# Keeping one product of a gated merge in its PSUM bank, in a one-core transformer-layer kernel

## The reference, cut to what matters

```python
z = rms_norm(x, g_mix) @ w_in                     # p, q, k, v, gate_pool, gate_attn
y_pool = pool_mixer(p, w_pool_grp, pool_scale) @ w_branch_pool
y_attn = window_attention(q, k, v, sinks) @ w_branch_attn
merged = sigmoid(gate_pool) * y_pool + sigmoid(gate_attn) * y_attn
x = x + merged @ w_out
x = x + peer_layer(rms_norm(x, g_ffn), ...)       # keys, top 16, 128 experts for each token
out = rms_norm(x, g_final)
```

## Time and profile before

| | |
|---|---|
| median of 3 runs | 2860.17 us |
| lowest and highest run | 2859.67, 2865.98 us |
| span of the profiled execution | 2856.4 us |
| merge loop, first pass | about 142 to 254 us |
| output projection, first pass | about 254 to 298 us |
| merge loop, second pass | about 542 to 653 us |
| output projection, second pass | about 653 to 699 us |

### The profile page before, as it was taken

The page is one execution under the profiler, slowest core; times in us unless marked ns, Lnnn a source line. Parts: engine busy times, 40 slices in busy tenths (PEclk is TensorE's granted clock), DMA queues, the critical chain, the costliest instruction groups (busy, mean ns, idle before and its releaser), DMA issues.

```text
span 2856.4 us, 39882 instructions
## 1 busy us (share of the span) xinstructions
PE 2772.4 (97%) x14843; PEld 2411.2 (84%) x14843; DVE 2332.4 (82%) x4690; ACT 964.2 (34%) x1505; POOL 2035.7 (71%) x1541
## 2 busy tenths in 40 slices
PE   8999999999998999999999999999999999999997
PEld 6688787687887888889988998999899989988996
DVE  2622798685899996888899998888898988989998
ACT  4432443324322996222222232222222222222222
POOL 5444478386786997687778777877677777778774
PEclk9999999999998999999999999999999999999999
DMA  4123422133323778899989988999899889989995
GB/s 155 46 88 96 170 75 82 40 105 107 107 92 123 227 231 300 306 346 348 339 324 358 345 330 332 351 348 335 322 350 345 330 338 343 353 315 361 336 349 205
DMA packets 267728, 717.90 MB, mean 251 GB/s; under 512 B 20880, under 2 KB 104208, under 8 KB 267536
## 3 DMA queue, kind: packets, MB, share of 16 engines
q0 software_dynamic: 110912, 403.75, 37.3%
q1 hardware_dynamic: 156624, 311.61, 32.4%
HBM read 657.86 MB, written 57.41 MB: 250 GB/s over the span
## 4 chain that ended last, share of the span: by engine, by line
PE 35%; DVE 6%; DMA 5%; POOL 2%; issue 1%; ACT 1%; DVEq 0%; SPq 0%; ACTq 0%
PE abank L1759 6%; PE abank L1761 6%; PE abank L1760 6%; PE ybank L1775 6%; PE ybank L1774 6%; PE ybank L1776 6%; DVE acc L1936 3%; DMA up<-in_up,e_idx 3%; DMA up<-in_down,e_idx 2%; DVE up L1924 1%; POOL tdown_lo L1706 1%; DVE e_y L2010 1%; POOL up L1699 1%; DMA w<-all_pre 1%; ACT tdown_hi L1800 0%
## 5 line engine op out<-in xcount | busy, mean ns | idle before, releaser
L1759 PE MATMUL abank<-m_hT,tdown_hi 128*128 128x384 f32 (+1 forms) x1856 | 579.4, 312 | 11.8 <-DVE w_lo L2002 6.8
L1761 PE MATMUL abank<-m_hT,tdown_lo 128*128 128x384 f32 (+1 forms) x1856 | 578.6, 312 | 0.0
L1760 PE MATMUL abank<-m_hlo,tdown_hi 128*128 128x384 f32 (+1 forms) x1856 | 577.7, 311 | 0.0
L1936 DVE SCALAR_TENSOR_TENSOR acc<-up,e_act,acc 128x1024 f32<-128x1024 f32 x381 | 489.8, 1286 | 70.0 <-DMA up<-in_up,e_idx 51.5
L1924 DVE CUSTOM_DVE_ANT_0 up<-up,acc 128x1024 f32<-128x1024 f32 x384 | 455.4, 1216 | 81.2 <-DMA up<-in_down,e_idx 80.6
L1774 PE MATMUL ybank<-tup_hi,w_hi 128*128 128x512 f32 x1280 | 503.5, 393 | 14.0 <-DVE w_lo L2002 10.5
L942 POOL TENSOR_TENSOR m_wlo<-m_raw,m_whi 128x1024 fp32r<-128x1024 f32 x128 | 311.5, 2442 | 288.2 <-ACT m_whi L719 284.6
L1775 PE MATMUL ybank<-tup_lo,w_hi 128*128 128x512 f32 x1280 | 502.7, 393 | 0.0
L1776 PE MATMUL ybank<-tup_hi,w_lo 128*128 128x512 f32 x1280 | 502.2, 392 | 0.0
L1699 POOL DMA_INDIRECT up<-in_down,e_idx x384 | 363.7, 947 | 99.1 <-issue 79.2
L1699 POOL DMA_INDIRECT up<-in_up,e_idx x384 | 362.2, 943 | 99.2 <-issue 80.6
(11 more groups left out here) (245 smaller groups left out, 4509.6 us busy)
## 6 DMA issues: line engine op xcount, KB each, us to landing
e_tup<-in_up SPq DMA_DIRECT2D x128, 512.0 KB, 5.5
m_raw<-in_tiles SPq DMA_DIRECT2D x116, 512.0 KB, 3.5
e_tdown<-in_downT SPq DMA_DIRECT2D x116, 512.0 KB, 5.5
gates<-all_table SPq DMA_DIRECT2D x64, 640.0 KB, 4.5
all_table<-t_out SPq DMA_DIRECT2D x9, 4096.0 KB, 14.6
m_raw<-in_downT SPq DMA_DIRECT2D x12, 512.0 KB, 3.8
up<-in_down,e_idx POOLq DMA_INDIRECT x384, 6.5
up<-in_up,e_idx POOLq DMA_INDIRECT x384, 6.5
```

The lines of the kernel that those rows point to most:

```text
L1759: nc.tensor.matmul(out, tdown_hi[:, q, at], h2T_hi[:, k, a:b], start=k == 0, stop=False)
L1760: nc.tensor.matmul(out, tdown_hi[:, q, at], h2T_lo[:, a:b, at], start=False, stop=False)
L1761: ins = nc.tensor.matmul(out, tdown_lo[:, q, at], h2T_hi[:, k, a:b], start=False, stop=k == KD - 1)
L1936: ins = nc.vector.scalar_tensor_tensor(out=acc[:], in0=src, scalar=act_of[:, b, k:k + 1], in1=acc[:], op0=ALU.mult, op1=ALU.add)
```

## The change

The product of the pool branch is written back to its own PSUM bank rather than to `sg[:, m % 2, 0]`. The sum is made in that bank too, and both the high and the low part of `merged` are taken from it. The product of the attention branch goes to `sg[:, m % 2, 1]` as before. Two waits follow from this. The bank of `bp` is now in use until the low part is taken, so its release is `m_low` and no longer `merged`. The sigmoids of step m overwrite what step m-2 had in `sg`, and that is now last read by the sum, so they wait for `merged` of step m-2 rather than for `m_low`.

```diff
         for m in range(KD):
             for i, name in enumerate(("gp", "ga")):
                 frees[name, m] = (sig_ready, 2 * m + 1 + i, 2 * KD) if m > 1 else (early_kept, 2 * m + 1 + i, TT)
-            frees["bp", m] = frees["ba", m] = (merged, m + 1, KD)
+            frees["bp", m] = (m_low, m + 1, KD)
+            frees["ba", m] = (merged, m + 1, KD)
...
-                    nc.scalar.activation(mhi(m), sg[:, m % 2, 0], ACT.Copy).then_inc(m_high, 1)
+                    nc.scalar.activation(mhi(m), bank("bp", m)[:], ACT.Copy).then_inc(m_high, 1)
...
                         if m >= 2:
                             wait_job(act, g, n, m)
-                            act.wait_ge(m_low, g * KD + m - 1)
+                            act.wait_ge(merged, g * KD + m - 1)
...
                 def merge_low(m):
                     dve.wait_ge(m_high, g * KD + m + 1)
-                    nc.vector.tensor_tensor(mlo[:, m], sg[:, m % 2, 0], mhi(m).bitcast(F32), ALU.subtract).then_inc(m_low, 1)
+                    nc.vector.tensor_tensor(mlo[:, m], bank("bp", m)[:], mhi(m).bitcast(F32), ALU.subtract).then_inc(m_low, 1)
 
                 for m in range(KD):
                     for i, n in enumerate(("bp", "ba")):
                         wait_job(dve, g, n, m)
                         dve.wait_ge(sig_ready, g * 2 * KD + 2 * m + 1 + i)
-                        mark(nc.vector.tensor_tensor(sg[:, m % 2, i], bank(n, m)[:], sg[:, m % 2, i], ALU.mult))
+                        to = sg[:, m % 2, 1] if i else bank(n, m)[:]
+                        mark(nc.vector.tensor_tensor(to, bank(n, m)[:], sg[:, m % 2, i], ALU.mult))
                     linked()
-                    nc.vector.tensor_tensor(sg[:, m % 2, 0], sg[:, m % 2, 0], sg[:, m % 2, 1], ALU.add).then_inc(merged, 1)
+                    nc.vector.tensor_tensor(bank("bp", m)[:], bank("bp", m)[:], sg[:, m % 2, 1], ALU.add).then_inc(merged, 1)
```

## The result

| | before | after |
|---|---|---|
| median of 20 runs | 2859.51 us | 2865.15 us |
| lowest to highest run | 2854.86 to 2865.98 us | 2861.14 to 2869.17 us |
| ratio to before, 95% interval | | 1.0023 [1.0016, 1.0029] |
| span of the profiled execution | 2856.4 us | 2859.4 us (its own time: 2861.44 us) |

By the medians the change makes the kernel slower by 5.6 us; the ratio stands for 6.6 us, its interval for 4.6 to 8.3 us. The forecast was 2865.3 us, no change within 0.3%, on the slow side. The profiled execution is the second shortest of the 20, so its span must not be set against the medians; what it is good for is the places.

What follows compares the result with a forecast made beforehand. TensorE's matmul stream was taken as the bound. Stalls of 0.88 and 2.53 us plus 1.70 us of clock gave 5.1 us, on a base of 2860.2 us: 2865.3 us, range 2859 to 2870 us.

Steps and rivals of the forecast that it cites:

- Nothing inside the loop: Merge loop, both passes: the new waits for low parts and the earlier sigmoids change nothing on TensorE, 0 us.
- First stall, 0.88 us: Start of first pass's output projection: output job (1,0) waits for low part 6, +0.88 us.
- Second stall, 4.06 us against 1.53 us: Second pass's output projection: job (1,0) waits 4.06 us for low part 6, replacing 1.53 us at job (3,0), +2.53 us.
- The clock, 1.70 us: Behind the second pass's stall: TensorE's granted clock dips once to the lower level, +1.70 us.
- rival B: End of second pass: VectorE arrives earlier; 2861.1 us if by 2.5 us, 2859.5 us if by 4.1 us; chance 0.14.
- PSUM operands at 0.69 us, free of GpSimd: Merge steps on VectorE: sum and low part with one operand in PSUM take 0.69 us, without waiting for GpSimd.
- Rival C: Both loop ends: sum and low part still wait for GpSimd; 9.5 us with a clock dip, 2869.7 us; chance 0.05.
- The sum, 5.1 us: TensorE's stream over both passes: 0.88 + 2.53 + 1.70 = 5.1 us longer in all.
- Slack behind it: Norm, turning, projections and the two stages after the output jobs: no slack, so the whole shift reaches the end.

Runs made afterwards that it cites:

- experiment 2: Changed kernel with low part 6 taken at the end of step 6, ahead of the products of step 7; 2858.82 us, ratio 0.9999 to before.
- experiment 6: Changed kernel with the output jobs at k = 0 alone in token order 0, 2, 1, 3; 2859.16 us, ratio 0.9995 to before.
- experiment 1: Kernel before with only the release of bp's bank moved from the sum to the low part, all data in SBUF; 2868.59 us, ratio 1.0034.
- experiment 3: Changed kernel with output jobs at k = 0 and 1 reordered, tokens 0 and 2 first, then 1 and 3; 2857.00 us, second timing 2856.07 us.
- 7: Changed kernel with low part 6 computed seven times in the second pass; 2868.53 us, ratio 1.0030 to before.
- 9: Changed kernel with low part 6 computed twice in both passes; 2864.53 us, ratio 1.0014 to before.
- experiment 4: Kernel before with output jobs at k = 0 and 1 reordered, tokens 0 and 2 first, then 1 and 3; 2859.05 us, ratio 0.9999.

## Why the prediction was right

*Nothing inside the loop.* Right: no wait for line 1292 but the two at the ends, and the freed sigmoids brought nothing.

*First stall, 0.88 us.* Measured 0.87 us in both profiles.

*Second stall, 4.06 us against 1.53 us.* Measured 3.80 and 3.82 us, so +2.3 in place of +2.5 us. The mechanism was right; the term was off by VectorE's arrival, which I had taken as fixed: it comes 2.53 us after TensorE's first output matmul now and came 2.78 us after it before. Its lookup instructions meet GpSimd's at slightly other moments (next to GpSimd's last weight copy it is the CAST of line 1164 that takes 2.40 us before, and now the later one of line 1169 that takes 2.32 us); this is rival B, at a tenth of its size.

*The clock, 1.70 us.* Right in both profiles of the changed kernel. That it was a forecast with a chance of its own was right too: experiment 2 kept its clock with 1.71 us of idle, 6 lost it with 2.27, and in 1 it stayed at 1.00 after 2.86 us in the first pass. But the row that the term was taken from proved less than I read out of it. TensorE starts the expert loop behind the same 2.84 us of idle in all 13 profiles of this study, and the clock fell behind it in six of them (among them before and the first profile after) and not in the other seven, as here in the second profile of experiment 3:

```profile
1101.19 0.36 PE L1763 MATMUL abank<-m_hT,tdown_hi 128*128 128x256 f32 x1 [2.84 <-PEq L1392]
...
1102.00:1107.00 5.00, 5.00 (x37) 1.00 1.14 346
```

For an idle stretch of 2.84 us the dip is a toss-up. Behind the longer stalls at (1,0) it came each time, 3.64 to 7.99 us in five profiles of five, so the term stands on the length of the stall; its size, 1.7 us, was the same in both places.

*PSUM operands at 0.69 us, free of GpSimd.* Right in 64 of 64, products included. By an estimate from the Trainium skill's larger fixed cost for a PSUM source (VectorE: DVE Perf Modes, section on the TRN2 errata), sum and low part would each have taken 0.065 us more; the sum took 0.700 us with all but one operand in PSUM against 0.691 us at least in SBUF, so the trace still does not agree. The Trainium skill (SBUF — State Buffer, section "SBUF: two separate sides") names as the VectorE instructions that take the port pair shared with GpSimd those in a 2-port mode and those with two SBUF inputs, the latter only against a GpSimd instruction that reads SBUF. The trace agrees: with one SBUF input 0.70 us at most, with two up to 2.97 us. Rival C, that they stay held, was wrong; its price was about right, since experiment 1 has it: 3.0 and 5.8 us late, 7.3 us more than before, where C had 5.2 + 2.6 = 7.8 us.

*The sum, 5.1 us.* The medians moved by 5.6 us. Terms as measured: 0.87 + 2.27 + 1.7 = 4.8 us. That the forecast of 2865.3 us met the median of 2865.15 us so closely is luck: the base of 2860.2 us, a median of three runs, was 0.7 us above that of 20 runs, and the sum 0.5 us below the difference.

*Slack behind it.* None was expected. The entry into the expert loop moved by 5.1 us in the first profile and 6.9 us in the second (1102.35, 1107.45, 1109.29), of which 0.8 and 0.2 us had come up before the first output projection, and the medians followed. Experiments 2, 3 and 6 take the loss back by order alone, 1 makes it larger, and 7 and 9 lengthen the stalls by as much as low part 6 is delayed: the cause is shown, not only argued. By the medians, undoing the stalls gave more than their terms: 6.0 us in experiment 6, 6.3 us in 2 and 8 to 9 us in 3, where the traces add up to 2.3, 4.3 and 6.4 us. The intervals are some 5 us wide. Stages A and B together, against the mean of the two profiles of the changed kernel, fell by 3.4, 4.5 and 6.7 us, which is nearer to the terms, so most of the excess is likely chance; whether all of it is stays open.

## What to carry over

A PSUM bank used as working space is released later, and the one who pays is the matmul job that opens it next, which may be in another stage: list for every bank who takes it over, and where the releasing instruction stands in its engine's queue. Where such a wait is the only harm, look for an order that opens that bank last, or that moves the releasing instruction up, before giving the change up; here both made the loss disappear. Busy time saved on an engine beside the path (25.6 us on VectorE here) is worth no more than TensorE's list of waits says, which here was 1.4 us for one sum.

## What the runs showed of the hardware

The granted clock fell during or right behind idle stretches of TensorE of 2.27, 3.64, 3.65, 4.34, 5.63 and 7.99 us and not behind 1.37, 1.71 and once 2.86 us; behind one and the same stretch of 2.84 us it fell in six profiles of 13. No sharp length shows, and what was lost on matmuls behind the stalls at (1,0) was 1.7 to 2.1 us whatever their length. Holding runs both ways: with the low parts of the merge read from two SBUF tiles (experiment 4), GpSimd's folding instructions beside them took 1.13 us on average and the last of them 0.85 us, where 0.99 and 0.30 us were enough with one operand in PSUM.
